# Two transformer blocks on one core: the order of the weight splits at the entry of the second block's mixers, and the units that carry w_ada tiles

## The reference

```python
c_act = jax.nn.silu(c)
for l in range(DEPTH_2):
    mod = (c_act @ w_ada[l] + b_ada[l]).reshape(B, 3, 3, D_MODEL)
    h = ada_norm(x, norm_g[l, 0], mod[:, 0, 0], mod[:, 0, 1])
    x = x + 0.5 * mod[:, 0, 2][:, None, :] * swiglu(h, ffn_w13[l, 0], ffn_w2[l, 0])
    h = ada_norm(x, norm_g[l, 1], mod[:, 1, 0], mod[:, 1, 1])
    x = x + mod[:, 1, 2][:, None, :] * token_mixer(h, w_in[l], ..., w_out[l], cos, sin)
    h = ada_norm(x, norm_g[l, 2], mod[:, 2, 0], mod[:, 2, 1])
    x = x + 0.5 * mod[:, 2, 2][:, None, :] * swiglu(h, ffn_w13[l, 1], ffn_w2[l, 1])
```

## Time and profile before

| | |
|---|---|
| median of 3 runs | 1745.72 us (1743.39 to 1750.4) |
| profiled execution | 1743.3 us |
| its span | 1741.5 us |
| TensorE (PE) busy | 1590.7 us, 91% |
| VectorE (DVE) busy | 1105.6 us, 63% |
| ScalarE (ACT) busy | 758.3 us, 44% |
| mean granted clock of TensorE | 0.957 |
| w_ada tiles on VectorE | 144, 1278 ns each |

### The profile page before, as it was taken

How to read it: one execution, slowest core, us unless ns; L and a number is a source line. 1 busy time by engine, 2 the same in 40 slices (tenths; PEclk the granted TensorE clock), 3 DMA queues, 4 the chain that set the end, 5 groups by cost and what they waited for, 6 DMA issues and landing times. The chain is left out here.

```text
span 1741.5 us, 24895 instructions
## 1 busy us (share of the span) xinstructions
PE 1590.7 (91%) x10338; PEld 1426.7 (82%) x10338; DVE 1105.6 (63%) x1569; ACT 758.3 (44%) x1142; POOL 22.9 (1%) x30
## 2 busy tenths in 40 slices
PE   5896879999999999789878999999997998789998
PEld 4684679999989998568668999899986686679996
DVE  3577646777776776557637676667765676366544
ACT  4634534444444443355525444354433554254441
POOL 0001000000000000000000000000000000000000
PEclk9998979999999999899889999999999998899999
DMA  6322326676765677344414677567663444046551
GB/s 251 121 97 103 119 73 241 251 284 262 276 230 203 252 265 263 121 163 164 158 37 155 233 277 267 192 229 258 244 254 130 175 164 158 25 156 247 190 186 43
DMA packets 56879, 327.31 MB, mean 188 GB/s; under 512 B 6448, under 2 KB 6832, under 8 KB 27312
## 3 DMA queue, kind: packets, MB, share of 16 engines
q1 hardware_dynamic: 55440, 322.76, 50.3%
q10 hardware_dynamic: 1328, 2.97, 0.5%
HBM read 324.65 MB, written 1.05 MB: 187 GB/s over the span
## 5 line engine op out<-in xcount | busy, mean ns | idle before, releaser
L286 DVE TENSOR_TENSOR wlo<-raw,whi 128x2048 fp32r<-128x2048 f32 (+2 forms) x236 | 534.0, 2265 | 315.9 <-ACT whi L281 315.6
L281 ACT ACTIVATE whi<-raw 128x2048 fp32r<-128x2048 f32 (+2 forms) x236 | 444.5, 1890 | 278.6 <-PE ps L1241 153.6
L1237 PE MATMUL ps<-hreg_r,whi 128*128 128x256 f32 x1760 | 501.3, 285 | 5.6 <-ACT mix L1286 5.6
L1241 PE MATMUL ps<-hreg_r,wlo 128*128 128x256 f32 x1760 | 500.0, 284 | 0.0
L1238 PE MATMUL ps<-hreg_r,whi 128*128 128x256 f32 x1760 | 500.0, 284 | 0.0
L1237 PEld LDWEIGHTS ps<-hreg_r,whi 128*128 128x128 f32 x1760 | 340.1, 193 | 7.0 <-ACT mix L1286 6.2
L1238 PEld LDWEIGHTS ps<-hreg_r,whi 128*128 128x128 f32 x1760 | 340.0, 193 | 0.5
L1241 PEld LDWEIGHTS ps<-hreg_r,wlo 128*128 128x128 f32 x1760 | 339.9, 193 | 0.0
L460 PE MATMUL ps<-whi,hreg_r 128*128 128x512 f32 (+2 forms) x352 | 149.8, 426 | 44.4 <-ACT whi L281 31.0
L1386 PE MATMUL ps<-whi,ireg_r 128*128 128x512 f32 x480 | 187.4, 390 | 0.5 <-ACT ireg_r L1352 0.5
L1387 PE MATMUL ps<-whi,ireg_r 128*128 128x512 f32 x480 | 187.0, 390 | 0.0
(11 more groups left out here) (341 smaller groups left out, 1709.6 us busy)
## 6 DMA issues: line engine op xcount, KB each, us to landing
raw<-in_wu SPq DMA_DIRECT2D x230, 1024.0 KB, 5.5
adaw<-in_wada SPq DMA_DIRECT2D x144, 512.0 KB, 4.3
raw<-in_wu SPq DMA_DIRECT2D x4, 568.0 KB, 4.6
raw<-in_wu SPq DMA_DIRECT2D x2, 544.0 KB, 4.9
x<-in_x SPq DMA_DIRECT2D x2, 512.0 KB, 4.4
out<-hreg SPq DMA_DIRECT2D x2, 512.0 KB, 2.6
crow<-in_c ACTq DMA_DIRECT2D x1, 512.0 KB, 4.0
greg<-in_cst ACTq DMA_DIRECT2D x1, 512.0 KB, 8.0
```

The costliest lines, as they stand in the source:

```text
L281: act.activation(self.whi[:, m, 0:width], self.raw[:, n % NRAW, 0:width], ACT.Copy).then_inc(*self.A.done("hi", n))
L286: dve.tensor_tensor(self.wlo[:, m, 0:width], self.raw[:, n % NRAW, 0:width], self.whi[:, m, 0:width].bitcast(F32), ALU.subtract).then_inc( ...
L1237: pe.matmul(o, wh, self.hhi[:, kt, :], start=kt == 0, stop=False)
L1241: mm = pe.matmul(o, wl, self.hhi[:, kt, :], start=False, stop=kt == 7)
```

## The change

In the entry of a mixer (`ns[0] == "m"`) both engines issue the splits of A's second and B's first half between the work of the two token halves, and the split of B's second half, which stood at the start of the mixer, in the ffn's last part: on ScalarE ahead of squares 1, on VectorE ahead of turned 1. TensorE's stream is the same. Other borders keep their order. In `ada_table` no tile is due in a stage's last four units (before: its last two), and the rate of the stages that are not mixers is 0.96 tiles a unit (before: 0.88). The total is 144 as before.

```diff
--- before.py
+++ after.py
@@ ada_table
-        elif at >= 3 and left > 2:
-            due += 60 if stage[n][0] == "m" else 88
+        elif at >= 3 and left > 4:
+            due += 60 if stage[n][0] == "m" else 96
@@ ffn_act
         ns, n = AFTER[st], UNIT[("w2", l, i), 8, 0]
         self.ahead_act(act, n)
         self.square_act(act, ns, 0)
+        if ns[0] == "m":
+            self.ahead_act(act, n + 1)
+            self.ahead_act(act, n + 2)
+            self.turned_act(act, ns, 0)
+            self.ahead_act(act, n + 3)
+            self.square_act(act, ns, 1)
+            self.turned_act(act, ns, 1)
+            return
@@ ffn_dve
             self.rstd_dve(dve, ns, t)
-            if t == 1 and ns[0] == "m":
-                self.ahead_dve(dve, n + 2)
+            if ns[0] == "m":
+                self.ahead_dve(dve, n + 1 + 2 * t)
             if ns == "end":
                 self.final_dve(dve, t)
             else:
                 self.turned_dve(dve, ns, t)
             if t == 0:
-                self.ahead_dve(dve, n + 1)
+                self.ahead_dve(dve, n + (2 if ns[0] == "m" else 1))
@@ mixer_act
-        self.ahead_act(act, n0)
         chunk("A", 4)
         chunk("B", 6)
@@ mixer_dve
-        self.ahead_dve(dve, n0)
         self.gate_rows_dve(dve, st, l, 1)
         self.ahead_dve(dve, n0 + 1)
```

## The result

The changed kernel takes 1721.29 us (median of 4 runs, 1719.89 to 1724.47), the kernel before 1745.95 us (4 runs, 1743.39 to 1750.4): a ratio of 0.9858, 95% interval 0.9836 to 0.988, so 1.4% faster and clear of the noise. The forecast was 1718, range 1710 to 1729, with 0.92 for a gain of over 0.5%. The profiled execution took 1719.9 us, against 1743.3 before and 1717.4 forecast for it: 23.4 us gained, 25.9 forecast. Between the medians the gain is 24.7 us.

What follows compares the result with a forecast made beforehand. TensorE, busy nine tenths of the span, was taken as the bound, with only its idle time, chiefly waits for B's late splits, winnable. 28.7 - 1.0 + 1.5 + 2.4 - 5.7 = 25.9 us off 1743.3 gives 1717.4, taken as 1718; range 1710 to 1729.

Steps and rivals of the forecast that it cites:

- entries of the mixers: Start of both mixers: splits moved ahead gain 15.3 and 13.4 us, 28.7 in all, less 1.0 for the clock.
- first layer's second ffn: Its border to the next ffn: without the tile ahead of the second token half's adds, the norm comes earlier; gain 1.5 us.
- second mixer to ffn: Border where calls 17 and 18 lose their tiles: wait of 3.66 us falls to 1.2; gain 2.4 us.
- mixers: Moved w_ada tiles lengthen waits inside both mixers: cost 5.7 us, bounds 0 and 19.
- The rival of a clock that stays low over the whole entry: Mixer entries: low clock throughout, 8 us less gain in both layers together, 1726 us; chance 0.10.
- the one by which the diagonal and the turned copies bind whatever is split first: Mixer entries: reordering splits gains nothing, only the tiles count, 1745 us; chance 0.05.
- the one by which B's raw tile is missing: Mixer entry: B's data not landed at its split at 712.3, so ScalarE blocks turned copies; slower, 1750 us; chance 0.02.
- Calls 10 to 11: Mixer tile moved from the split issued at n0 + 10 to n0 + 11: cost 1.3 us in the first mixer.
- call 9: Tile at the split issued at n0 + 9 in the second mixer: cost 0.5 us.
- call 16: Tile moved from call 15, in both mixers, ahead of the copy a TensorE wait needs: cost 1.3 us each.
- Call 14: New tile in the second mixer, ahead of the copy that the wait at 1459.22 needs: cost 1.3 us.
- The wait that I expected to lengthen at the first L1947: First mixer, L1939 before the change: TensorE's wait was to grow by 1.3 us.

Runs made afterwards that it cites:

- the order alone: The changed kernel with the old table of w_ada tiles (last two units free, rate 0.88): 1723.33 us, ratio 0.9867.
- the table alone: The kernel before, with its old order of splits, given the new w_ada table: 1751.18 us, ratio 1.0025.
- the shifted pair: The changed kernel and the kernel before, each with 14 unused fp32 matmuls added in the first ffn: 1720.41 and 1749.7 us, single executions.
- the shifted kernel of before: The kernel before with 14 unused fp32 matmuls added in the first layer's first ffn, so all later work starts later: 1749.7 us, single execution.

## Why the prediction was right

By its own steps, profile against profile, in us gained:

```
                              forecast    measured
entries of the mixers         28.7 - 1.0  15.5 + 13.5 = 29.0
first layer's second ffn      1.5         1.1
second mixer to ffn           2.4         2.2
mixers                        -5.7        -3.6 - 4.7 = -8.3
all before the first mixer    0           -0.6
sum                           25.9        23.4
```

- **The entries** came out as replayed, within 1.3 us of 28.7 less 1.0. A did not wait for turned copies: their last low half ended at 719.52, 2.3 us after A's start (forecast: 2.3 after), B's low half made TensorE wait 0.62 us (forecast 1.0), the diagonal 1.99 (2.2), and L1979, 29.6 us after A's start (29.8), waited 0.54 us (1). The clock, for which I took 1 us off, fell for only 3.4 us in each entry. The rival of a clock that stays low over the whole entry fell: 0.94. So did the one by which the diagonal and the turned copies bind whatever is split first (putting back the second split alone costs 16.6 us) and the one by which B's raw tile is missing (the split started at 713.00 with the slot).
- **The border of the two ffns** gave 1.1, though its wait hardly moved, 1.75 to 1.67 us. The norm's operand comes 1.2 us sooner, as the tile is gone, and TensorE is there 1.0 us sooner, as its last matmuls ahead of the wait ran at 2.4 GHz and no longer at 1.2. The sum was near, by the operand alone; that the wait hardly moved is the clock's doing.
- **The second mixer's border** gave 2.2. The wait fell from 3.66 to 2.08 us, not to 1.2, and 3.4 us less ran at the low clock. That the total is near 2.4 is in part luck: the forecast had all of it as wait.
- **The mixers** are the term that was mis-sized, -8.3 for -5.7. Ahead of w_out2 they lost 2.0 and 3.2 us, close to the forecast. Calls 10 to 11 cost 0.9 in each mixer, in the second with call 9 (forecast 1.3 and 0.5); call 16 cost 1.2 in each (1.3), seen as 4.86 for the 3.66 and 3.65 us of L2081. Call 14 was to cost 1.3 in the second. Its wait grew from 3.38 to 5.82 us, by more than forecast, but TensorE had come earlier, since an earlier wait had shrunk from 2.74 to 1.54 us and 2.1 us less ran at 1.2 GHz: the stretch up to the wait's end took 15.9 us both times. The longer wait then told behind it, 1.0 us by 3.6 us more at 1.2 GHz. The other 3.1 us are the low clock in both w_out2, for which the forecast had no term. They do not hang on the tiles: w_out2 lost 3.0 us with the order alone, which has the old tiles, and 4.3 with the table alone. Nor are they a mere accident of the two profiles, as the shifted pair differs by 8.4 us in the mixers too. By which step the change brings them about stays open.
- The wait that I expected to lengthen at the first L1947 stayed at 2.74 us; in its place a wait of 0.73 us for ScalarE's exponentials appeared 3.6 us ahead of it. The place was right, the waiter was not.
- **Two sums** in the forecast's reasons do not come out, and nothing hung on them. With each late us costing one a layer, the change would turn to a loss with a landing after 712.3 + 1.5 + 25.9 / 2 = 726.8, not 729, and a landing at 732 would give 1754 us, not 1750. And with the mixers absorbing all and 5 us at the ffn's entry its own terms reach 1718 - 5.7 - 2.6 = 1709.7, not 1711.
- **The range** held. What the reasons for it lacked is the spread of single executions ahead of the first mixer, 3.3 us between two profiles of one kernel, which is larger than either border term.

## What to carry to other kernels

Read the engines' timelines side by side, and look for a long instruction queued behind one that waits while its engine was idle earlier; moving it there costs only what it delays of the next consumer, and a replay with the durations of the rows gave that to 1 us in 29. A wait of TensorE can be worth more than its length: behind the 5.57 us here the matmuls ran at 1.2 GHz, and of the 8.6 us 2.0 were slower matmuls. Count background work by the stage that can hide it: 15 tiles of 1.28 us cost 0.8 each inside the mixers, clock included, and nothing that the stretches show inside the ffns. And before a loss to the low clock in one stretch is called an accident, shift both kernels and compare the sums over the whole stage.

## What the runs showed of the hardware

- After one and the same wait (3.38 or 3.39 us) TensorE went on at 2.4 GHz or fell to 1.2. In the first mixer of the shifted kernel of before, the wait (3.38 us) and all that leads up to it from the gate rows on (134.2 us against 134.1) are as in the kernel before, and what differs, as far as the trace shows, is the moment; w_out2 took 28.1 us there and 26.5 before. TensorE at the start of w_out2, first before, then after:

```profile
895.81 0.47 PE L460 MATMUL ps<-whi,hreg_r 128*128 128x512 f32 x1 [3.38 <-DVE an L2294]
...
896.57 0.39 PE L460 MATMUL ps<-whi,hreg_r 128*128 128x512 f32 x1
...
882.89 0.47 PE L460 MATMUL ps<-whi,hreg_r 128*128 128x512 f32 x1 [3.39 <-DVE an L2301]
...
883.82 0.63 PE L460 MATMUL ps<-whi,hreg_r 128*128 128x512 f32 x1
```

  In the second pair the matmuls go from 0.39 to 0.63 us each. The clock falls 0.6 us behind the wait here and 1.2 us behind it in the first mixer of the shifted kernel of before, amid dense matmuls; in that kernel's second mixer it had fallen 1.3 us before the wait ended. The 3.4 us at 1.2 GHz in the changed kernel cost 1.6.
- The first 207 us of one program ran 23.9 us at 1.2 GHz in one execution and 44.4 in another, 3.3 us apart. The Trainium skill, "TensorE: Matmul & The Clock Gate", Part 1, says that the number of matmuls that run at the low clock at the start of a kernel differs from run to run of one kernel; these two profiles agree, with 23.9 and 44.4 us.
- 14 fp32 matmuls of 128x128 stand in the trace as 28 rows and take 3.1 to 3.2 us, twice what I had put on them.
